# Earlier cumulative sums and 64-column first products in the blocked inverse of an RWKV-7 stage (hybrid two-layer decoder trunk, fp32, one core)

## The reference, cut to what matters

```python
# State (B,H,N_v,N_k):
# S_t = S_{t-1} diag(decay_t) + (S_{t-1} a_t) b_t^T + v_t k_t^T ;  y_t = S_t r_t
def step(state, inp):
    r_t, w_t, k_t, v_t, a_t, b_t = inp
    sa = jnp.einsum('bhvk,bhk->bhv', state, a_t)
    state = state * w_t[:, :, None, :] + sa[..., None] * b_t[:, :, None, :] + v_t[..., None] * k_t[:, :, None, :]
    y = jnp.einsum('bhvk,bhk->bhv', state, r_t)
    return state, y
```

## Time and profile before

| | |
|---|---|
| three runs | 1919.58 us median (1919.21 to 1921.1) |
| the profiled execution, its own time | 1919.7 us |
| its span, first to last instruction | 1917.9 us |
| busy share of the span | PE 97%, PE weight loads 49%, DVE 30%, ACT 24%, POOL 9% |
| mean granted TensorE clock | 0.993 |
| the four chunks of the RWKV stage | from about 201 us to about 361 us of the span |

### The profile page before, as it was taken

How to read it: one execution, slowest core, us unless ns; L and a number is a source line. 1 busy time by engine, 2 the same in 40 slices (tenths; PEclk the granted TensorE clock), 3 DMA queues, 4 the chain that set the end, 5 groups by cost and what they waited for, 6 DMA issues and landing times.

```text
span 1917.9 us, 21821 instructions
## 1 busy us (share of the span) xinstructions
PE 1866.6 (97%) x8174; PEld 930.2 (49%) x8174; DVE 575.3 (30%) x1048; ACT 464.3 (24%) x810; POOL 177.2 (9%) x216
## 2 busy tenths in 40 slices
PE   8999999999999999999999999999999999999997
PEld 4555888646453333333334443686463333333333
DVE  2154556342141322313133103311241322313223
ACT  3245343332331111111113014323331111111113
POOL 2000333020100000000001000121100000000001
PEclk8999999999999999999999999999999999999999
DMA  6210100035079999999996112204079999999993
GB/s 188 88 45 0 45 1 1 11 107 214 1 288 423 423 423 424 423 422 423 424 423 231 45 44 91 86 1 179 0 293 422 423 424 423 423 423 422 423 424 138
DMA packets 88414, 465.77 MB, mean 243 GB/s; under 512 B 22303, under 2 KB 24463, under 8 KB 47402
## 3 DMA queue, kind: packets, MB, share of 16 engines
q1 hardware_dynamic: 77600, 450.98, 58.0%
q0 software_dynamic: 4608, 7.92, 1.1%
q10 hardware_dynamic: 6154, 6.15, 1.0%
HBM read 467.59 MB, written 6.29 MB: 247 GB/s over the span
## 4 chain that ended last, share of the span: by engine, by line
PE 81%; DMA 11%; DVE 4%; ACT 1%; POOL 1%; issue 1%; SPq 0%; DVEq 0%; POOLq 0%; ACTq 0%
PE ps L1036 75%; DMA W<-in_moe_w 11%; PE ps L1242 2%; PE ps L1705 1%; PE ps L1676 1%; DVE memN L1827 0%; DVE XI L2013 0%; PE ps L1179 0%; PE ps L1466 0%; DVE XJ L1954 0%; PE ps L1049 0%; DVE gcs L2122 0%; DVE KKt L1987 0%; DVE XT L2294 0%; DVE gsn L2153 0%
## 5 line engine op out<-in xcount | busy, mean ns | idle before, releaser
L1036 PE MATMUL ps<-W,xgT 128*64 128x512 f32 x2048 | 453.9, 594 | 6.5 <-DMA W<-in_moe_w 5.2
L1036 PE MATMUL ps<-HT,W 128*128 128x512 f32 (+2 forms) x896 | 340.7, 537 | 4.9 <-DVE XT L1834 1.7
L1036 PEld LDWEIGHTS ps<-W,xgT 128*64 128x64 f32 x2048 | 143.6, 137 | 287.4 <-issue 272.0
L1036 PEld LDWEIGHTS ps<-HT,W 128*128 128x128 f32 (+1 forms) x896 | 167.4, 190 | 167.2 <-issue 152.6
L2281 DVE TENSOR_TENSOR XT<-ps,XT 128x512 f32<-128x512 f32 x240 | 165.9, 691 | 239.9 <-PE ps L1036 239.9
L1036 PE MATMUL ps<-W,act 128*64 128x512 f32 x1024 | 231.9, 595 | 0.0
L1036 PE MATMUL ps<-spread,ysb 128*128 128x512 f32 x512 | 228.3, 599 | 2.2 <-issue 2.2
L2273 DVE TENSOR_TENSOR act<-ps,sl 128x256 f32<-128x256 f32 x64 | 26.8, 419 | 446.1 <-ACT sl L987 446.1
L1036 PEld LDWEIGHTS ps<-spread,ysb 128*128 128x128 f32 x512 | 94.7, 190 | 135.3 <-issue 134.9
L1036 PEld LDWEIGHTS ps<-W,act 128*64 128x64 f32 x1024 | 70.6, 137 | 133.4 <-issue 133.4
L983 ACT ACTIVATE hs<-ps 128x512 f32<-128x512 f32 x64 | 38.2, 597 | 387.3 <-PE ps L1036 387.3
(11 more groups left out here) (409 smaller groups left out, 1719.3 us busy)
## 6 DMA issues: line engine op xcount, KB each, us to landing
W<-in_moe_w SPq DMA_DIRECT2D x256, 1024.0 KB, 17.4
W<-in_moe_w SPq DMA_DIRECT2D x64, 2048.0 KB, 17.9
W<-in_od_w_in SPq DMA_DIRECT2D x6, 2048.0 KB, 8.3
W<-in_ev_w_in SPq DMA_DIRECT2D x3, 2048.0 KB, 7.7
W<-in_xa_wq SPq DMA_DIRECT2D x2, 2048.0 KB, 8.8
W<-in_xa_wo SPq DMA_DIRECT2D x2, 2048.0 KB, 11.9
hrows<-hk ACTq DMA_DIRECT2D x8, 512.0 KB, 12.0
W<-in_od_w_out SPq DMA_DIRECT2D x2, 2048.0 KB, 10.0
```

The lines of the kernel that those rows point to most:

```text
L1036: return te.matmul(o, l, r, start=first, stop=last)
```

## The change

`ck_kt` is a new semaphore. BT now signals ck_el, and KT signals ck_kt, on POOL and in chunk 0 on DVE; PE waits for ck_kt after the first transposition of open_chunk, DVE's last chunk waits for ck_kt. ACT runs `decays(c + 1)` at level 3, ahead of the AKV copy. DVE runs fc, all four scans and mid ahead of level 1. The first product covers the even blocks' 64 columns, except in chunk 0, level 1, and ACT copies its result into the even blocks of UL alone.

```diff
@@ gpsimd
-                        g.tensor_tensor(BT[:, :, :], At[:, :, t], Em[:, :, :], ALU.mult)
+                        g.tensor_tensor(BT[:, :, :], At[:, :, t], Em[:, :, :], ALU.mult).then_inc(s["ck_el"], 1)
                     if following:
-                        g.tensor_tensor(KT[:, :, :], Kt[:, :, t], Em[:, :, :], ALU.mult).then_inc(s["ck_el"], 1)
+                        g.tensor_tensor(KT[:, :, :], Kt[:, :, t], Em[:, :, :], ALU.mult).then_inc(s["ck_kt"], 1)
@@ scalar
-                            sc.activation(UL[r][:, :, :].rearrange("p j t -> p (j t)"), ps[:, r, :], ACT.Copy).then_inc(s["iv_ul"], 1)
+                            Uf = UL[r][:, :, :].rearrange("p j t -> p (j t)")
+                            if c == 0 and l == 1:
+                                sc.activation(Uf, ps[:, r, :], ACT.Copy).then_inc(s["iv_ul"], 1)
+                            else:
+                                sc.activation(halves(Uf, l)[0], ps[:, r, 0:256].rearrange("p (b w) -> p b w", w=1 << l),
+                                              ACT.Copy).then_inc(s["iv_ul"], 1)
                         if l == 3:
+                            if c + 1 < NCH:
+                                decays(c + 1)
                             act.wait_ge(s["akv_done"], c + 1)
                             sc.activation(AKV[:, :], ps[:, 3, :], ACT.Copy).then_inc(s["akv_in"], 1)
-                        if l == 4 and c + 1 < NCH:
-                            decays(c + 1)
@@ tensor
                     turn_chunk(c, 1)
+                    pe.wait_ge(s["ck_kt"], c + 1)
...
-                                ins = mm(ps[:, r, j * P:j * P + P], MA_[:, j, r, 0, :], XI[r][:, j, :])
+                                if c == 0 and l == 1:
+                                    ins = mm(ps[:, r, j * P:j * P + P], MA_[:, j, r, 0, :], XI[r][:, j, :])
+                                else:
+                                    ins = mm(ps[:, r, j * HD:j * HD + HD], MA_[:, j, r, 0, :], halves(XI[r][:, j, :], l)[0])
@@ vector
-                def cumulate(t, CS=CS, which=range(4)):
+                def cumulate(t, CS=CS):
-                    for j in which:
+                    for j in range(4):
                         ins = ve.tensor_tensor_scan(CS[:, j, :], ones[:, :], SGt[:, j, t], 0.0, ALU.mult, ALU.add)
-                    if j == 3:
-                        st.then(ins)
-                        ve.tensor_copy(mid.unsqueeze(2), CS[:, :, CH // 2 - 1:CH // 2]).then_inc(s["ck_scan"], 1)
+                    st.then(ins)
+                    ve.tensor_copy(mid.unsqueeze(2), CS[:, :, CH // 2 - 1:CH // 2]).then_inc(s["ck_scan"], 1)
...
                 for c in range(NCH):
                     following = slice((c + 1) * CH, (c + 2) * CH)
                     if c + 1 == NCH:
-                        dve.wait_ge(s["ck_el"], NCH)
+                        dve.wait_ge(s["ck_kt"], NCH)
...
+                    else:
+                        dve.wait_ge(s["ck_exp"], c + 1)
+                        st.then(ve.tensor_copy(fc.unsqueeze(2), Ep[:, :, CH - 1:CH]))
+                        cumulate(following)
                     for l in range(1, CORNER):
...
-                        if l == 1 and c + 1 < NCH:
-                            dve.wait_ge(s["ck_exp"], c + 1)
-                            st.then(ve.tensor_copy(fc.unsqueeze(2), Ep[:, :, CH - 1:CH]))
-                            cumulate(following, which=(0, 1))
-                        if l == 2 and c + 1 < NCH:
-                            cumulate(following, which=(2, 3))
```

More of the change, by code:

```diff
@@ L337, in trunk @@
             "shifted", "lora_done", "lora_taken", "kk_max", "pre_a", "pre_p", "post_v", "post_a", "post_p", "gate_done", "gate_in", "bonus_sum", "bonus_p", "bonus_in", "half_done", "half_in",
-            "ck_scan", "ck_mid", "ck_cs", "ck_rh", "ck_sn", "ck_exp", "ck_el", "ck_vc", "ck_turned", "ck_tok", "ck_mat", "ck_masked", "ck_kmat", "ck_kraw", "ck_kmask", "ck_sd", "ck_y", "ck_y_in", "ck_s",
+            "ck_scan", "ck_mid", "ck_cs", "ck_rh", "ck_sn", "ck_exp", "ck_el", "ck_kt", "ck_vc", "ck_turned", "ck_tok", "ck_mat", "ck_masked", "ck_kmat", "ck_kraw", "ck_kmask", "ck_sd", "ck_y", "ck_y_in", "ck_s",
             "iv_id", "u_first", "u_mid", "u_cross", "u_part", "iv_u", "iv_ul", "iv_v", "iv_x", "akv_done", "akv_in", "u_done", "u_in",
@@ L1938, in even @@
                 ve.tensor_tensor(AR[:, :, 0, :], KKt[:, :, first], Dp0[:, :, :], ALU.mult)
-                ve.tensor_tensor(BT[:, :, :], At[:, :, first], Em0[:, :, :], ALU.mult)
-                ve.tensor_tensor(KT[:, :, :], Kt[:, :, first], Em0[:, :, :], ALU.mult).then_inc(s["ck_el"], 1)
+                ve.tensor_tensor(BT[:, :, :], At[:, :, first], Em0[:, :, :], ALU.mult).then_inc(s["ck_el"], 1)
+                ve.tensor_tensor(KT[:, :, :], Kt[:, :, first], Em0[:, :, :], ALU.mult).then_inc(s["ck_kt"], 1)
                 shift(12)
```

## The result

The changed kernel took 1930.92 us in the median of 6 runs (1928.14 to 1935.8) against 1920.41 us (1919.21 to 1921.88) for the kernel before. The medians are 10.5 us apart; the ratio is 1.0061, with a 95% interval of 1.0051 to 1.0071, or some 11.7 us. So the kernel is about 11 us slower, where the prediction said 2.3 us less. The profiled execution took 1935.8 us and was the slowest of the six, 16.1 us above the profiled execution of before; what the profile shows as lost is more than the median has.

The account below looks back on a forecast made before the run. PE, 81% busy, was taken to bound the kernel through its chain of waits. Terms -5.5 - 0.3 + 2.7 + 0.8 = -2.3 us gave 1917.3 us; range 1913.7 to 1919.9.

Parts of the forecast that it names:

- The waits: PE's idle time for POOL's KT before score_beta, ending chunks 0, 1 and 2, all goes: gain 5.5 us.
- The copies of 256 columns: ACT's shorter UL copy saves 0.07 us in level 5 of four chunks, hidden in levels 1 to 4: gain 0.3 us.
- The rival of slow short runs: ACT's UL copies in levels 1, 2, 4 and 5 write short runs slowly, kernel about 1924 us; chance 0.06.
- The scans: Ahead of level 1, DVE takes turns with POOL's masks: loss 2.7 us in chunk 0, 0.8 in chunks 1 and 2.
- The 64-column products: First products of the levels: weight loads set the pace, 1.86 us per sixteen either way, so PE gains nothing.
- the hole: Gap of 2.6 us that the moved scans open in chunk 0, where the clock might fall.
- rival 4: TensorE's clock falls at the scans' gap in chunk 0, giving back about 2 us: 1919.3 us; chance 0.06.

Follow-up runs that it names:

- the kernel with 128 columns and no hole: Changed kernel with 128-column first products, scans back behind levels 1 and 2, decays after the AKV copy; 1913.83 us, ratio 0.9963.
- the narrow kernel: Changed kernel, 64-column first products kept, scans back behind levels 1 and 2, decays after the AKV copy; 1934.11 us, ratio 1.0083.
- one-run form: Changed kernel, scans and decays moved back, first products taking the tile's first 64 columns instead of every second block; 1932.7 us, ratio 1.0050.

## Why the prediction was wrong

**The waits (5.5 us, right).** All three went. The chunk that ran at full clock went from 40.89 to 38.92 us: 1.97, of which 1.83 is the wait. The split signal alone gives 3.65 in the stage; the kernel with 128 columns and no hole, 5.4 in the stage and 5.6 in the median.

**The copies of 256 columns (0.3 us, right in kind).** They took 0.38 us, 0.44 and 0.40 in level 1, where runs are shortest. The rest of that chunk's gain, 0.14 us, is twice the 0.07 counted. The rival of slow short runs is out. (Its figure of 0.15 us for the placing's short runs is 0.45 - 0.27 = 0.18; nothing hangs on it.)

**The scans (2.7 us in chunk 0, right; 0.8 in chunks 1 and 2, wrong).** The four scans beside POOL's masks took 3.42 us, the placing came 2.6 us late, as the rows on weighted_keys and copy_predicated had it. mid took its turn as well, but it just fitted into DVE's idle time, so 0.8 should have been 0. With the Trainium skill's exclusive lock (SBUF — State Buffer, "Who interferes with whom") these rows agree.

**The 64-column products (costed at nothing; this step failed).** It is true that the 16 loads take the same 1.86 us, in the chunk at full clock. So PE gained nothing in time. But with the columns taken away the clock fell, and with columns put back in either product it held. The step priced PE's time and put the clock at nothing, without a reason. In the profiled execution chunk 2 took 51.1 us instead of 38.9, 12.2 us lost. Chunk 0 took 39.1 where 32.5 - 1.8 + 2.6 = 33.3 was due, 5.8 us lost, the hole's dip among them. That loss is no work of the hole: without one the narrow kernel's chunk 0 took 36.8 us and the wide one's 30.7, 6.1 apart. Against a net gain of some 3 us (5.5 + 0.3 - 2.6) these give the sign.

**The clock (rival 4, mis-sized and misplaced).** The prediction named a fall of the clock, tied it to the hole alone, priced it at 2 us and gave it 0.06. The hole does bring a dip, about 2.6 us in the profile of the kernel with 128 columns (chunk 0 35.9 instead of 33.3), and chunk 0 is free of it in the two 128-column kernels without the hole. The large fall came from elsewhere, in a chunk where PE was busy nearly all the time. The row behind this rival was also misread. It speaks of some 8 us with little work ahead of 1406; the rows of those 8 us have PE busy 3.39 and 2.58 of 4 us:

```profile
1398.00:1402.00 4.00, 3.39 (x32) 2.86 (x30) 2.98 (x17) 2.66 (x4) 0.00 (x0) 1.00 1.01 422
1402.00:1406.00 4.00, 2.58 (x22) 2.35 (x22) 2.45 (x18) 2.79 (x4) 0.00 (x0) 1.00 1.04 408
```

So the trace of before already had a fall without an idle stretch of that length ahead of it. It also ran its products of 128 and of 64 columns at one pace, so half of the first products' streaming was to go in the same time. I read that as free.

The Trainium skill (TensorE: Matmul & The Clock Gate, "What's actually happening") says that the throttled state is the default and that recent activity releases it. That activity bears on the clock, these runs show. But PE's rows read 4.00 of 4.00 us in windows at 0.50, and 39.10 of 41 us in the kernel before at 1.00 against 40.65 at 0.71 in the narrow kernel without a hole, so the busy time of the profile alone did not foretell the level.

**Range.** It was 1913.7 to 1919.9, and the measured 1930.9 lies 11 us above it. Slower by over 0.2% had a chance of 0.05, all of it for ACT's copies, which were not slow. The same change with the second product widened lies in the range (1917.2). That this is next to the forecast's 1917.3 is partly luck: it has a dip of the clock in chunk 0 that the sum left out, and not the 0.8 us for mid that the sum had.

## What to carry to other kernels

A matmul whose pace is set by its weight load can have columns removed at no gain, and with enough of them removed from a stretch the clock may fall and the whole stretch pay for it, here 3.53 us for 16 loads instead of 2.24; look at the granted clock of such a stretch first, and leave unused columns in if they are free. Split a semaphore so that it releases its reader at the last operand that the reader really needs: that alone gave here 3.65 of the 5.4 us that the stage gained with earlier decays and half copies added, and by the medians (1913.95 and 1913.83 us) the two kernels can't be told apart. In this kernel DVE instructions with two SBUF inputs should not be put beside a run of POOL instructions, unless DVE has idle time to absorb a turn per instruction.

## What the runs showed of the hardware that was not expected

- The clock fell with PE 3.86 and 3.78 of 4 us busy and stayed at 0.50 for 30 us with PE at 4.00 of 4.00, and with columns added whose results are thrown away it held: 1934.1 us with 64 and 64 columns, 1914.5 with 64 and 128, 1913.8 with 128 and 64, 1912.6 with one half of the first products narrow.
- Narrow kernels differ much between executions: 1930.7 to 1950.2 us in 4 executions of the narrow products alone, 1922.9 to 1934.7 in 5 of the one-run form, where the kernel before stayed within 1917.5 and 1922.1 in all 59.
- A DVE copy of four elements per partition from SBUF to SBUF waits for POOL like a large one: 1.06 us instead of 0.17.
